# Chunk 2 of the scan between the z-row products, and the z gate on GpSimd by Exp, Ln and Exp

## What is computed

```python
y = y_f + rev(y_b) + xs * d_skip[:, None]          # y_f, y_b: y_diag + y_off, over chunks of 128
o_c = rmsnorm(y * silu(z), ssm_g)                  # z: 512 columns of the projection
y_off = einsum('bclhn,bchpn,bhcl->bclhp', cm, h_enter, exp(cs))
```

## Time and profile before

| | us |
|---|---|
| median of 3 runs | 777.74 |
| lowest, highest | 777.46, 777.85 |
| the profiled execution's own time | 776.89 |
| its span, first to last instruction | 775.1 |
| TensorE (matmul) busy in the span | 739.2 |
| VectorE busy | 581.7 |
| ScalarE busy | 506.7 |
| GpSimd busy | 50.4 |

### The profile page before, as it was taken

The page is one execution under the profiler, slowest core; times in us unless marked ns, Lnnn a source line. Parts: engine busy times, 40 slices in busy tenths (PEclk is TensorE's granted clock), DMA queues, the critical chain, the costliest instruction groups (busy, mean ns, idle before and its releaser), DMA issues.

```text
span 775.1 us, 10981 instructions
## 1 busy us (share of the span) xinstructions
PE 739.2 (95%) x4020; PEld 574.3 (74%) x4020; DVE 581.7 (75%) x965; ACT 506.7 (65%) x842; POOL 50.4 (7%) x36
## 2 busy tenths in 40 slices
PE   4999999899999999999999999989999999999995
PEld 2557877458966788888879788745798788888884
DVE  3258386987666789999868746879766789999975
ACT  3049694485456778778756678557556887787754
POOL 0001342000000000000000125200000000000000
PEclk9999999999999999999999999999999999999998
DMA  9963033977338799999865112186731199999912
GB/s 364 425 253 110 7 129 140 424 269 309 110 114 356 281 380 375 366 372 367 304 241 218 55 55 82 55 345 250 290 148 55 55 330 368 374 366 374 371 42 85
DMA packets 33630, 186.22 MB, mean 240 GB/s; under 512 B 5152, under 2 KB 6560, under 8 KB 16544
## 3 DMA queue, kind: packets, MB, share of 16 engines
q1 hardware_dynamic: 33568, 185.42, 63.1%
HBM read 182.79 MB, written 2.62 MB: 239 GB/s over the span
## 4 chain that ended last, share of the span: by engine, by line
PE 76%; DVE 11%; ACT 7%; issue 4%; DMA 1%; DVEq 0%; ACTq 0%; SPq 0%
PE psum L890 23%; PE psum L1050 11%; PE psum L919 11%; PE psum L1252 5%; PE psum L1017 4%; PE psum L720 3%; PE psum L951 3%; PE psum L868 2%; DVE att L2310 1%; PE psum L1222 1%; PE psum L1120 1%; ACT split L1452 1%; PE psum L771 1%; PE psum L903 1%; PE psum L1134 1%
## 5 line engine op out<-in xcount | busy, mean ns | idle before, releaser
L2099 DVE TENSOR_TENSOR split<-ring,split 128x2048 fp32r<-128x2048 f32 x96 | 219.9, 2290 | 28.3 <-ACT split L1583 26.9
L1583 ACT CAST split<-ring 128x2048 fp32r<-128x2048 f32 x96 | 183.6, 1912 | 23.8 <-PE psum L919 14.4
L890 PE MATMUL psum<-split,y_hi 128*128 128x512 f32 x512 | 162.0, 398 | 0.4 <-ACT selT L1556 0.4
L890 PEld LDWEIGHTS psum<-split,y_hi 128*128 128x128 f32 x512 | 94.5, 190 | 18.9 <-issue 0.4
L890 PE MATMUL psum<-split,y_lo 128*128 128x512 f32 x256 | 100.8, 394 | 0.0
L1050 PE MATMUL psum<-ring_r,hT_hi 128*128 128x512 f32 x216 | 73.2, 393 | 0.0
L919 PE MATMUL psum<-split,hidT 128*128 128x512 f32 x256 | 69.4, 393 | 0.0
L919 PEld LDWEIGHTS psum<-split,hidT 128*128 128x128 f32 x256 | 47.3, 188 | 12.1 <-DVE hidT_lo L2104 2.5
L890 PEld LDWEIGHTS psum<-split,y_lo 128*128 128x128 f32 x256 | 48.4, 189 | 10.3
L2541 POOL TENSOR_TENSOR ud<-const,da_hi 128x1024 fp32r<-128x1024 f32 x12 | 27.3, 2294 | 395.3 <-DVE da_lo L2200 387.9
L1050 PEld LDWEIGHTS psum<-ring_r,hT_hi 128*128 128x128 f32 x216 | 40.0, 188 | 9.0 <-issue 0.8
(11 more groups left out here) (319 smaller groups left out, 1429.8 us busy)
## 6 DMA issues: line engine op xcount, KB each, us to landing
ring<-in_w_gu SPq DMA_DIRECT2D x64, 1024.0 KB, 5.1
ring<-in_w_ada SPq DMA_DIRECT2D x40, 1024.0 KB, 6.7
ring<-in_w_down SPq DMA_DIRECT2D x32, 1024.0 KB, 5.2
ring<-in_w_rows SPq DMA_DIRECT2D x12, 1024.0 KB, 4.7
ring<-in_first SPq DMA_DIRECT2D x8, 1024.0 KB, 15.3
ring<-in_w_out SPq DMA_DIRECT2D x8, 1024.0 KB, 5.1
ring<-in_w_xbc SPq DMA_DIRECT2D x8, 800.0 KB, 9.2
par<-in_par SPq DMA_DIRECT2D x1, 1728.0 KB, 13.6
```

The lines of the kernel that those rows point to most:

```text
L890: last = pe.matmul(dst, x[:, g, t, :], w[:, j, :], start=(t == 0 and i == 0), stop=(t == KD - 1 and i == 2))
L1583: act.copy(splits[unit_split(n)][:, 0, :], slot(key)).then_inc(raised("whi", l, p), 1)
L2099: tt(lo, slot(unit_key(l, p, n)), hi.bitcast(F32), ALU.subtract).then_inc(raised("wlo", l, p), 1)
```

## The change

The step list: `ssm_y(2)` moves from behind the three products `rows(5, m)` to between the first and the second, and both `ssm_off` steps move from among the attention steps to between the second and the third. `silu_z` goes. In its place come, for each tile m, `gate_in(m)` and `gate_sigmoid(m)`: ScalarE computes exp(-z), GpSimd takes the minimum with 1e30 and adds 1, ScalarE takes Ln and then Exp(-x), which is the sigmoid, and GpSimd multiplies it with z. The multiplication of `y` by the gate moves from VectorE to GpSimd. `gate_norm` now waits for each tile's product instead of for all. The PSUM banks of the moved steps are given by hand (`beyond_rows`).

```diff
@@ layer_steps
-    s += [("rows", 5, m) for m in range(TILES)] + [("ssm_y", 2), ("silu_z",)]
+    s += [("rows", 5, 0), ("ssm_y", 2), ("gate_in", 0), ("rows", 5, 1), ("gate_in", 1), ("gate_sigmoid", 0), ("ssm_off", 1), ("ssm_off", 2), ("rows", 5, 2), ("gate_sigmoid", 1)]
     burst = 6 if l else 3
     s += ada[early:burst]
     heads = head_steps()
+    at = heads.index(("scores", 1))
+    heads[at:at] = [("gate_in", 2)]
     at = heads.index(("scores", 2))
-    heads[at:at] = [("ssm_off", 1)]
-    at = heads.index(("scores", 3))
-    heads[at:at] = [("ssm_off", 2)]
+    heads[at:at] = [("gate_sigmoid", 2)]
@@ build
+            with ExitStack() as after_last_state:
+                z_exp = sb("z_exp", [P, TILES, DS], c=after_last_state)
             xs = sb("xs", [P, DS], c=mix)
...
+        def beyond_rows(l, n):
+            return (uses["row", l, 0, 2][0] + n) % 7
@@ TensorE
-                        pe.wait_ge(*fill(("ydiag", l, m)))
+                        pe.wait_ge(*fill(("ydiag", l, m), beyond_rows(l, 1) if m == 2 else None))
...
-                        pe.wait_ge(*fill(("state", l, m)))
+                        pe.wait_ge(*fill(("state", l, m), beyond_rows(l, 2) if m == 2 else None))
...
-                            pe.wait_ge(*fill(("yoff", l, m, g)))
+                            pe.wait_ge(*fill(("yoff", l, m, g), beyond_rows(l, (5, 6, 0, 1)[2 * m - 2 + g])))
...
+                        turn[0] = beyond_rows(l, 1)
@@ ScalarE
-                    elif kind == "silu_z":
-                        for m in range(TILES):
-                            act.wait_ge(*taken(("row", l, m, 2)))
-                        act.activation(z, z, ACT.Silu).then_inc(sig["zs"], 1)
-                        act.preload_act_table_set("natural_log_exp_and_others")
+                    elif kind == "gate_in":
+                        m = arg[0]
+                        act.wait_ge(*taken(("row", l, m, 2)))
+                        act.wait_ge(*full(("ydiag", l, 2)))
+                        act.wait_ge(*full(("state", l, 2)))
+                        act.activation(z_exp[:, m, :], z[:, m, :], ACT.Exp, scale=-1.0).then_inc(sig["zexp"], 1)
+                    elif kind == "gate_sigmoid":
+                        m = arg[0]
+                        act.wait_ge(sig["zone"], per["zone"] * l + m + 1)
+                        act.activation(z_exp[:, m, :], z_exp[:, m, :], ACT.Ln).then_inc(act_step, 1)
+                        act.wait_ge(act_step, act_steps())
+                        act.activation(z_exp[:, m, :], z_exp[:, m, :], ACT.Exp, scale=-1.0).then_inc(sig["zsig"], 1)
@@ VectorE
-                    elif kind == "gate":
-                        dve.wait_ge(sig["zs"], per["zs"] * l + 1)
-                        dve.wait_ge(*taken(("ydiag", l, 0)))
-                        m = arg[0]
-                        ins = tt(y[:, m, :], y[:, m, :], z[:, m, :], ALU.mult)
...
@@ GpSimd
+                    if step[0] == "gate_in":
+                        m = step[1]
+                        pool.wait_ge(sig["zexp"], per["zexp"] * l + m + 1)
+                        pool.tensor_scalar(z_exp[:, m, :], z_exp[:, m, :], 1e30, 1.0, ALU.min, ALU.add).then_inc(sig["zone"], 1)
+                    elif step[0] == "gate_sigmoid":
+                        m = step[1]
+                        pool.wait_ge(sig["zsig"], per["zsig"] * l + m + 1)
+                        tt(z[:, m, :], z[:, m, :], z_exp[:, m, :], ALU.mult).then_inc(sig["zs"], 1)
+                    elif step[0] == "gate":
+                        m = step[1]
+                        pool.wait_ge(sig["zs"], per["zs"] * l + m + 1)
+                        if m:
+                            pool.wait_ge(sig["ysum"], per["ysum"] * l + m)
+                        else:
+                            pool.wait_ge(*taken(("ydiag", l, 0)))
+                        tt(y[:, m, :], y[:, m, :], z[:, m, :], ALU.mult).then_inc(sig["yz"], 1)
```

More of the change, by code:

```diff
@@ L1778, in _ @@
                     elif kind == "gate_norm":
-                        act.wait_ge(sig["yz"], per["yz"] * l + 1)
                         for m in range(TILES):
+                            act.wait_ge(sig["yz"], per["yz"] * l + m + 1)
                             ins = act.activation(tmp[:, m, :], y[:, m, :], ACT.Square, accum_out=nrm[:, 24 + m:25 + m])
@@ L2299, in _ @@
                         ym = y[:, m, :].rearrange("p (g n) -> p g n", g=2)
-                        for d in range(2):
-                            tt(ym, ym, tmp[:, 0:2, d * 256:(d + 1) * 256], ALU.add).then_inc(dve_step, 1)
-                            dve.wait_ge(dve_step, dve_steps())
+                        tt(ym, ym, tmp[:, 0:2, 0:256], ALU.add).then_inc(dve_step, 1)
+                        dve.wait_ge(dve_step, dve_steps())
+                        tt(ym, ym, tmp[:, 0:2, 256:512], ALU.add).then_inc(sig["ysum"], 1)
+                        dve.wait_ge(sig["ysum"], per["ysum"] * l + m)
                     elif kind == "scores":
```

4 lines of the change are left out of this document (1 added, 3 removed).

## The result

The changed kernel takes 784.37 us (median of 4 executions, 781.57 to 786.77) against 777.6 us for the kernel before in the same session: ratio 1.0090, 95% interval 1.0067 to 1.0113. Run again in another session it took 782.58 us, ratio 1.0065 (1.0042 to 1.0088). The forecast said 779.6 us, 776.4 to 781.8: the sign was right, the size was missed on the high side, outside the range.

What follows compares the result with a forecast made beforehand. TensorE, busy 95%, bounds the kernel; only its idle time, 8.1 us at most, could be gained. Layer 0 +2.1 and layer 1 -0.2 give +1.9 on 776.89, so 778.8; plus 0.85 to the median, 779.6 us, range 776.4 to 781.8.

Steps and rivals of the forecast that it cites:

- the end of the z rows releases the slots 4.6 us later: Both layers: moved scan steps delay the last z-row product, so the next weight pieces are issued 4.6 us later.
- The relief wins: Rival, both layers: weights not late, lighter VectorE gains 1.8 us in layer 0 and 3.0 in layer 1; 772.9 us, chance 0.12.
- Layer 0, +2.1 forecast: Layer 0 attention: late weights delay ada_turn by 2.4 us, 0.31 us of later idle time goes; sum +2.1 us.
- piece 7 at 149.8: Layer 0 attention: this weight piece lands and starts at 149.8 us against 147.24, so 2.6 us late.
- Layer 1, -1.2 to +0.8 forecast: Layer 1: turn(2) +0.1 or +1.7 us, less 0.9 to 1.3 of further waits; -1.2 to +0.8, middle -0.2.
- turn(2) starts at 521.0 or 522.6, against 520.93: +0.1 or +1.7: Layer 1 attention: turn(2) follows a weight piece landing at 517.0 or 518.6 us, so starts 0.1 or 1.7 us later.
- I take off 0.9 to 1.3: Layer 1 after turn(2): VectorE without the three gates (2.0 us) cuts TensorE's further waits by 0.9 to 1.3 us.
- A place where both engines share SBUF: At hin, both layers: GpSimd's first min-and-add might hold VectorE's state scaling, costing TensorE 0 to 0.35 us each; 0 taken.
- GpSimd's products of about 1.05 us that nobody waits for: Sign that the forecast is right: GpSimd's products take about 1.05 us and no engine waits for them.
- Priced at 1.05: Inside attention: Ln on ScalarE waits 1.05 us for GpSimd's min-and-add, the price of a 512-column product; hidden in layer 0.
- rival 3: Attention: Ln of tile 2 waits for GpSimd ahead of turn_qk's copies, deciding once GpSimd exceeds 1.5 us; 781.2 us, chance 0.10.
- At full clock: Both layers, from scan's end to attention's end: TensorE's idle times, 3.5 and 4.6 us, were taken at full clock.

Runs made afterwards that it cites:

- with the old gate: Scan steps moved as in the change, but Silu gate on VectorE and both ssm_off behind the last z-row product; 779.97 us, 1.0035 against the kernel before.
- four placements: Kernel before, old gate, one or both ssm_off moved: both behind last z row, both ahead of scores, only tile 1's there (two versions); 1.0054, 1.0086, 1.0054, 1.0072.

## Why the prediction was wrong, point by point

**Right: what bounds the kernel, and what moves the weights.** The step "the end of the z rows releases the slots 4.6 us later" held. SyncE's timeline, and the ring's issues and landings in after:

```profile
133.98 14.69 SPq L1375 DMA_DIRECT2D ring<-in_w_ada  x9
```

```profile
L1375 SPq DMA_DIRECT2D ring<-in_w_ada x4: 328/379/432, 134.0 to 135.9; - x4
...
DMA to landing us min/median/max: 4.8/8.1/10.6
```

The first issue is 10.23 us after the first z copy (133.98 - 123.75), against 5.45 before (130.24 - 124.79): 4.8 later. The four landings took 4.8, 6.9, 9.2 and 10.6 us; the earlier trace rows had 4.8 and 6.9. TensorE idled 3.6 us for weights in layer 0 (forecast about 3.9) and 2.45 in layer 1 (forecast 2.6). The kernel with late weights alone shows that this is enough to lose. It isn't shown to be all: with the old gate and 1.7 us of waits for weights instead of 5.7 the time stayed (1.0035 against 1.0043). "The relief wins" fell too: with no weight late, four placements lost as well.

**Layer 0, +2.1 forecast, +3.26 measured.** The failed term is the landing of piece 7: "piece 7 at 149.8", from a pace carried over from before. It started at 150.15 with the first z copy 1.04 us earlier, so at 151.2 on the forecast's scale, 1.4 late; it was issued at 136.7 and landed 13.4 us later, at 150.1, 3.6 us after the one before (135.9 + 10.6 = 146.5) and not 2.7. `ada_turn` was 3.6 us later than before, where 2.4 was forecast, and the end 3.3. The relief itself came as forecast: turn(2) has no wait. The held scale is visible in this layer but not paid, as the kernel with the y products on VectorE shows.

**Layer 1, -1.2 to +0.8 forecast, +1.99 measured.** The pieces landed on the earlier of the two forecast times (517.3 on the forecast's scale against 517.0). The step "turn(2) starts at 521.0 or 522.6, against 520.93: +0.1 or +1.7" failed: it started 2.9 us late (526.46 - 502.31 = 24.15 against 520.93 - 499.71 = 21.22). Without the held scale by the y products and at full clock the same step was +0.8, inside the forecast. So 2.1 us of it are the hold and the clock; with the clock full and the hold kept it was +2.55. That puts about 1.7 us on the hold and 0.4 on the clock. The trace of after agrees: alone, the scale would have ended 1.73 us sooner, and TensorE's 1.55 us at turn(1) would be gone. The step had neither in it; it took turn(1)'s scale at its old length. The last step held: from there to the end after gained 0.9 us, and "I take off 0.9 to 1.3" was meant for the three gates; with the gates back on VectorE that gain is gone (+0.15). The ground for it was misread, though: of layer 1's smaller waits, 2.5 us and not 2.7, only 1.2 are for VectorE and the rest for ScalarE.

**The port.** "A place where both engines share SBUF" looked at one place, `hin`, priced it 0 to 0.35 and took 0; that price was right, since the products behind it started on time (128.90 us, no wait). The place that cost was the y products: "GpSimd's products of about 1.05 us that nobody waits for" is false. The earlier trace rows had shown the effect (1.21 us for a VectorE product of 384 columns), and the gates' new place had never been laid beside VectorE's softmax.

**GpSimd's min-and-add.** Priced at 1.05, it took 1.99 us, over the 1.5 at which rival 3 was said to decide. Ln did wait 1.32 us for it, yet TensorE didn't: without the instruction the time stayed (1.0062 against 1.0065). The price was wrong, and the place of its cost too.

**The clock.** "At full clock" was assumed all through. Of the 18 profiled executions of after and the variants that can be read, 15 had a granted clock under 0.9 in at least one stretch of 5 us early in attention; before had none there. It also moves the median against the profiled execution: the forecast put it 0.85 us above the profiled execution, and it was 2.8 above in the first session and 0.3 in the second.

**The sum.** The median came out 4.8 us over the forecast. In rounded parts, 2.2 of it are layer 1, 1.2 layer 0, and 2.0 the larger distance of the median from the profiled execution, which goes with the clock; the parts outside the stretches take off 0.7. The direction came from the late weights, as forecast. The steps that failed are the landing of piece 7, turn(2) in layer 1 with a scale that nothing holds, and the full clock.

What stays open: why the clock falls in some executions and not in others of the same program, how much of each variant's loss would stay at full clock, and whether ScalarE's nine activations cost anything by themselves.

## What to carry to other kernels

A step that is moved takes its place in every queue: ask on TensorE what it filled, on VectorE what now stands behind it, and on the DMA queue whose buffer it holds. Here each new place paid in one of the three: the waits changed their names, and their sum in the two stretches grew from 8.0 us to between 9.1 and 12.7 in the kernels whose traces were read. Work given to an idle GpSimd isn't free while VectorE is on the critical path: lay its instructions beside VectorE's in time, and keep them out of a stretch whose small VectorE instructions are waited for.

## What was not expected of the hardware

- A VectorE instruction of 128 x 2 elements took 0.93 and 1.23 us instead of 0.17 and 0.16 beside a GpSimd product, and a pair of 0.48 us took 2.21 across two of three back-to-back products, each of its halves ending 0.1 us behind a product. Beside GpSimd's min-and-add a VectorE addition of two 128 x 512 tensors kept its 0.69 us.
- GpSimd's instruction with a constant operand on 512 columns took 1.57 us with one operation and 1.99 with two, while its product of two tensors took 1.05 to 1.27.
- Idle times of 2.45 and 2.42 us at the same place were followed by a granted clock of 0.76 in one kernel and 1.00 in the other. Executions of one program at mean clocks of 0.997 and of 0.987 to 0.989 lay 5 us apart.
